# Two unread gaps beside the ring of weights in a two-model float32 kernel

## The chip, the cores and the metric

The kernel runs on one NeuronCore of a Trainium2 chip. The metric is device time in microseconds of one execution, less is better. A time is the median of several runs; for the kernel before, three runs gave 3114.55 us (3114.27 to 3118.92).

## The reference, cut to what matters

Two stacks of two layers each work on one sequence of 256 rows of 1024 numbers in float32. A layer of the first stack is a gated feed-forward block, a mixer with four branches (two convolutions, two kinds of attention), and another feed-forward block; a layer of the second is a feed-forward block, a mixer with windowed attention and a gated delta rule, and another feed-forward block. What is computed around this change is always the same:

```python
normed = norm(h)                         # 256 x 1024
f = (silu(normed @ w_gate) * (normed @ w_up)) @ w_down
u = normed @ w_in                        # some 9,000 columns, then the mixers
```

## The kernel before, in words

Every product with weights is made from three matmuls of a reduced float32 form (float32r). A weight w is held as a high part and a low part (w minus high), an activation likewise, and the product is high x high + high x low + low x high; PARTS in line 1258 is this list.

All weights come through a ring of four slots (SLOTS, UNIT: 2048 floats, 8192 bytes per partition). SyncE loads a unit into a slot of `weight_ring` when TensorE has given the slot back (line 1064, semaphore slots_free). ScalarE copies it, rounded, into the same slot of `weights_high` (line 1837, called from split_high). VectorE, for some units GpSimd, subtracts that from the ring and writes the difference in place, under the name `weights_low` (lines 2177 and 1144): `weight_ring` and `weights_low` are one stretch of memory. Then TensorE reads both parts. Each engine's instructions stand in an order fixed when the program is built, by a plan (PLANS) that also says how far ahead the parts of the next units are made.

The normed rows stand transposed in `normed_t_high` and `normed_t_low` (XT), 8 blocks of 256 columns. Most matmuls multiply a 128x128 block of weights, held stationary in the array after a weight load (LDWEIGHTS), with 256 moving columns of the normed rows. That is so in `cols_product` (line 1264, gate and up), `product` (line 1431, the wide projections) and line 1655 (gates of the branches). In lines 1313 and 1448 the roles are exchanged: the normed rows are stationary, the weights move. In lines 1658 and 1661 the weights are stationary and the moving columns lie in `work_parts`, the split outputs of the mixers. In lines 1373 and 1399 (the down projections) blocks of `work_parts` are stationary and 512 columns of weights move.

A row of the profile names the moving operand first, and then the stationary one: `psum<-normed_t_high,weights_low` has moving normed rows and a stationary block of the low part.

Memory is given out in the order of the declarations, so the places are known. Within a partition (in bytes): `residual` 8192, `normed_t_high` 8192, `normed_t_low` 8192, `weight_ring` (= `weights_low`) 32768, `weights_high` 32768, `feature_rows` 8192, `params` 1916 rounded up to 1920, `constants` 7680, `small` 2128 rounded up to 2144, and `work` (= `work_parts`) 102400. Before the change the normed rows, the low and the high parts start at the same place modulo 512 bytes, and blocks of them are 512 or 1024 bytes long; `work` starts 480 bytes further (8192 + 1920 + 7680 + 2144 = 19936, which is 38 x 512 + 480).

Of the kernel before, what the change touches and what calls it, by code (L numbers as in the profile page):

```python
# [13 lines left out]
P = 128  # L14
# [728 lines left out]
def build_kernel(nc, x, stream1, stream2, prms, feat1, feat2, con, onehot, rowmask, relb, toep, out):  # L743
    with ExitStack() as ctx:
        def sb(name, shape):
            return ctx.enter_context(nc.sbuf_tensor(name, shape, F32))

        def sb_twice(name, parts, shape):


            with nc.sbuf_tensor(name, shape, F32) as whole:
                pass
            return whole, ctx.enter_context(nc.sbuf_tensor(parts, shape, F32R))
# [7 lines left out]
        XTL = ctx.enter_context(nc.sbuf_tensor("normed_t_low", [P, KB, S], F32R))  # L761
        XT = (XTH, XTL)

        RING, LOW = sb_twice("weight_ring", "weights_low", [P, SLOTS, UNIT])
        HIGH = ctx.enter_context(nc.sbuf_tensor("weights_high", [P, SLOTS, UNIT], F32R))
        PG = sb("feature_rows", [P, 2, D])
        PRM = sb("params", [P, max(NCOL1, NCOL2)])
# [195 lines left out]
        def reach(key, k):  # L963
            done = sum(LAYERS[b] * PLANS[b].count.get(key, 0) for b in range(now.blk))
            return CREDIT.get(key, 0) + done + now.l * PLANS[now.blk].count.get(key, 0) + k
# [35 lines left out]
        def loaded_at(i):  # L1001

            return reach(("slot", i % SLOTS), 16 * (i // SLOTS + 1))

        def low_sem(i):
            pl, i, _ = unit_plan(i)
            return low_by_pool if pl.by[i] == "pool" else low_by_vector

        def low_at(i):
            pl, i, following = unit_plan(i)  # L1010
            name = "low_by_" + pl.by[i]
            return reach(name, pl.low_at[i] + following * PLANS[now.blk].count.get(name, 0))

        def some(tile, i, q, n):
            w = width(i) // QUARTERS
            return tile[:, i % SLOTS, q * w:(q + n) * w]
# [59 lines left out]
        def _(pool):  # L1076
# [60 lines left out]
            def split_low(i, q, n):  # L1137

                if low_sem(i) is low_by_pool:
                    pool.wait_ge(high_ready, reach("high_ready", QUARTERS * i + q + n))  # L1140
                    w = width(i) // QUARTERS // 2
                    for part in range(2 * q, 2 * (q + n)):
                        at = (slice(None), i % SLOTS, slice(part * w, (part + 1) * w))
                        ins = pool.tensor_tensor(LOW[at], RING[at], HIGH[at].bitcast(F32), ALU.subtract)  # L1144
                        if part % 2:
# [87 lines left out]
        def _(pe):  # L1233
# [14 lines left out]
            def weights(st, a, wait=True):  # L1248

                i = PLANS[now.blk].place[st.unit]  # L1250
                if wait:
                    pe.wait_ge(low_sem(i), low_at(i))
                n = width(i)
                return [v.rearrange("p (a b) -> p a b", a=a)
                        for v in (HIGH[:, i % SLOTS, 0:n], LOW[:, i % SLOTS, 0:n])]

# [120 lines left out]
            def last_rows(st, t, u, key, stop):  # L1377
# [14 lines left out]
                if t == 0:  # L1392
                    pe.wait_ge(low_sem(i), low_at(i))
                w = [v[:, i % SLOTS, :].rearrange("p (a b) -> p a b", a=2) for v in (HIGH, LOW)]
                for n in range(2):
# [439 lines left out]
        def _(act):  # L1835
            def copy(dst, src, scale=1.0):
                return act.activation(dst, src, ACT.Copy, scale=scale)  # L1837
# [13 lines left out]
            def split_high(i, q, n):  # L1851

                act.wait_ge(slot_loaded[i % SLOTS], loaded_at(i))
                copy(some(HIGH, i, q, n), some(RING, i, q, n)).then_inc(high_ready, n)

# [303 lines left out]
        def _(dve):  # L2159
# [13 lines left out]
            def split_low(i, q, n):  # L2173

                if low_sem(i) is low_by_vector:
                    dve.wait_ge(high_ready, reach("high_ready", QUARTERS * i + q + n))
                    dve.tensor_tensor(some(LOW, i, q, n), some(RING, i, q, n), some(HIGH, i, q, n).bitcast(F32),  # L2177
                                      ALU.subtract).then_inc(low_by_vector, n)
# [647 lines left out]
```

## Time and profile before

| What | Value |
|---|---|
| median of three runs | 3114.55 us |
| span of the profiled execution, first to last instruction | 3111.1 us |
| TensorE matmul busy | 2998.3 us (96%), 22114 matmuls |
| TensorE weight load busy | 2829.8 us (91%) |
| VectorE / ScalarE / GpSimd busy | 61% / 43% / 17% |
| DMA, queue of the weights | 43.0% of 16 engines, 471.95 MB |
| mean granted TensorE clock | 0.991 |

The profiled execution has no time of its own beside its span; the median of the runs is 3.4 us above the span. Matmuls are pipelined: the 0.28 us shown for one matmul is how long it is under way, while its successor starts after 0.12 us. What counts is therefore the step from one start to the next in the timeline.

### The profile page before, as it was taken

To read this page: it belongs to the slowest core of one execution; us is meant where nothing else is said; L and a number is where in the kernel's file an instruction comes from. 1 tells how busy PE (TensorE), PEld (TensorE's weight loads), DVE (VectorE), ACT (ScalarE), POOL (GpSimd) and SP (SyncE) were. 2 spreads that over 40 slices of the span, in tenths; PEclk is the share of its full clock that TensorE was granted. 3 is DMA by queue.
4 is the path that set the end of the run, shared out by engine and by line. 5 is a ranking of instruction groups with operands and counts; after the bars stand their busy time and mean duration, and the time that the engine had idled before them with its cause. 6 is when DMAs were issued, how large, how long until landed. Compare 5 with 4: busy or idle time off the path is not lost.

```text
span 3111.1 us, 54768 instructions
## 1 busy us (share of the span) xinstructions
PE 2998.3 (96%) x22114; PEld 2829.8 (91%) x22114; DVE 1909.5 (61%) x3367; ACT 1348.0 (43%) x2281; POOL 522.1 (17%) x821
## 2 busy tenths in 40 slices
PE   7999999999999999999999998999999999899998
PEld 7999999898999999898998888989989888889897
DVE  5557876656556876655655467466565556664655
ACT  4345454434334454434434543434343355443432
POOL 1000000000000000000002554550000056556000
PEclk9999999999999999999999999999999999999999
DMA  6554445555554456554563322255545533123553
GB/s 226 181 185 163 144 146 180 188 188 181 185 175 177 142 171 176 195 188 176 197 217 136 105 86 77 79 185 180 201 173 216 183 109 109 69 82 137 179 196 130
DMA packets 72861, 498.66 MB, mean 160 GB/s; under 512 B 8320, under 2 KB 8496, under 8 KB 19872
## 3 DMA queue, kind: packets, MB, share of 16 engines
q1 hardware_dynamic: 67824, 471.95, 43.0%
q0 software_dynamic: 4512, 22.20, 2.4%
q8 instruction: 176, 2.88, 0.4%
q10 hardware_dynamic: 272, 0.99, 0.1%
q14 instruction: 77, 0.63, 0.1%
HBM read 490.92 MB, written 4.19 MB: 159 GB/s over the span
## 4 chain that ended last, share of the span: by engine, by line
issue 47%; PE 37%; DVE 7%; POOL 3%; ACT 2%; DVEq 1%; DMA 1%; POOLq 1%; ACTq 0%
PE psum L1264 11%; PE psum L1431 7%; PE psum L1373 4%; PE psum L1655 4%; POOL weights_low L1144 2%; PE psum L1313 2%; DMA weight_ring<-stream 1%; PE psum L1658 1%; PE psum L1661 1%; DVE work L2580 1%; PE psum L1399 1%; DVE weights_low L2177 1%; PE psum L1551 1%; ACT weights_high L1837 1%; PE psum L1771 1%
## 5 line engine op out<-in xcount | busy, mean ns | idle before, releaser
L1837 ACT ACTIVATE weights_high<-weight_ring 128x2048 fp32r<-128x2048 f32 (+5 forms) x774 | 907.5, 1189 | 851.0 <-DMA weight_ring<-stream 850.8
L2177 DVE TENSOR_TENSOR weights_low<-weight_ring,weights_high 128x2048 fp32r<-128x2048 f32 (+5 forms) x528 | 896.4, 1704 | 612.7 <-ACT weights_high L1837 610.5
L1264 PE MATMUL psum<-normed_t_high,weights_high 128*128 128x256 f32 x2560 | 725.1, 283 | 0.0
L1264 PE MATMUL psum<-normed_t_high,weights_low 128*128 128x256 f32 x2560 | 723.9, 283 | 0.0
L1264 PE MATMUL psum<-normed_t_low,weights_high 128*128 128x256 f32 x2560 | 723.9, 283 | 0.0
L1264 PEld LDWEIGHTS psum<-normed_t_high,weights_high 128*128 128x128 f32 x2560 | 490.6, 192 | 3.6 <-issue 0.6
L1264 PEld LDWEIGHTS psum<-normed_t_low,weights_high 128*128 128x128 f32 x2560 | 490.7, 192 | 3.0
L1264 PEld LDWEIGHTS psum<-normed_t_high,weights_low 128*128 128x128 f32 x2560 | 490.7, 192 | 0.0
L1144 POOL TENSOR_TENSOR weights_low<-weight_ring,weights_high 128x256 fp32r<-128x256 f32 x544 | 400.8, 767 | 230.9 <-ACT weights_high L1837 230.8
L1431 PE MATMUL psum<-normed_t_high,weights_high 128*128 128x256 f32 x1248 | 384.4, 308 | 9.2 <-DVE weights_low L2177 9.2
L1431 PE MATMUL psum<-normed_t_low,weights_high 128*128 128x256 f32 x1248 | 355.1, 285 | 0.0
L1431 PE MATMUL psum<-normed_t_high,weights_low 128*128 128x256 f32 x1248 | 354.5, 284 | 0.0
L1373 PE MATMUL psum<-weights_high,work_parts 128*128 128x512 f32 x1088 | 341.7, 395 | 0.0
L1431 PEld LDWEIGHTS psum<-normed_t_high,weights_high 128*128 128x128 f32 x1248 | 241.3, 193 | 22.6 <-issue 16.4
L1431 PEld LDWEIGHTS psum<-normed_t_low,weights_high 128*128 128x128 f32 x1248 | 241.6, 194 | 0.8
L1431 PEld LDWEIGHTS psum<-normed_t_high,weights_low 128*128 128x128 f32 x1248 | 240.6, 193 | 0.0
L1373 PEld LDWEIGHTS psum<-weights_high,work_parts 128*128 128x128 f32 x1088 | 199.3, 188 | 43.6
L1655 PE MATMUL psum<-normed_t_high,weights_high 128*128 128x256 f32 x768 | 232.2, 302 | 4.0 <-POOL weights_low L1144 4.0
L1655 PE MATMUL psum<-normed_t_low,weights_high 128*128 128x256 f32 x768 | 217.5, 283 | 0.0
L1655 PE MATMUL psum<-normed_t_high,weights_low 128*128 128x256 f32 x768 | 217.3, 283 | 0.0
L1373 PE MATMUL psum<-weights_low,work_parts 128*128 128x512 f32 x544 | 214.9, 395 | 0.0
L1399 PE MATMUL psum<-weights_high,work_parts 128*128 128x512 f32 x576 | 182.0, 397 | 0.4 <-DVE weights_low L2177 0.4
(279 smaller groups left out, 4578.5 us busy)
## 6 DMA issues: line engine op xcount, KB each, us to landing
weight_ring<-stream SPq DMA_DIRECT2D x400, 1024.0 KB, 4.8
weight_ring<-stream SPq DMA_DIRECT2D x64, 768.0 KB, 4.2
feature_rows<-feat POOLq DMA_DIRECT2D x12, 1024.0 KB, 5.2
work<-toeplitz_rows POOLq DMA_DIRECT2D x8, 512.0 KB, 6.6
toeplitz_rows<-work POOLq DMA_DIRECT2D x16, 192.0 KB, 3.9
params<-prms POOLq DMA_DIRECT2D x5, 239.5 KB, 3.0
residual<-x SPq DMA_DIRECT2D x2, 512.0 KB, 4.2
out<-residual SPq DMA_DIRECT2D x4, 256.0 KB, 2.0
```

The lines of the kernel that those rows point to most:

```text
L1144: ins = pool.tensor_tensor(LOW[at], RING[at], HIGH[at].bitcast(F32), ALU.subtract)
L1264: ins = pe.matmul(PS[:, bank, at:at + S], w[a][:, first + k, c * P:(c + 1) * P], src[b][:, k, :], start=(k, m) == (0, 0), stop=(k, m) == ( ...
L1313: ins = pe.matmul(PS[:, job.bank, t * S:(t + 1) * S], XT[low][:, k, t * P:(t + 1) * P], w[part][:, k, :], start=n == 0, stop=n == len(FIRS ...
L1373: ins = pe.matmul(PS[:, b, :], src[c][:, r, t * P:(t + 1) * P], w[a][:, r, n * HALF:(n + 1) * HALF], start=start and m == 0, stop=False, s ...
L1399: ins = pe.matmul(PS[:, b, :], src[c][:, r, t * P:(t + 1) * P], w[a][:, r, n * HALF:(n + 1) * HALF], start=False, stop=stop and (r, m) == ...
L1431: ins = pe.matmul(PS[:, job.bank, c * S:(c + 1) * S], w[i][:, k, c * P:(c + 1) * P], XT[j][:, k, :], start=(k, m) == (0, 0), stop=(k, m) = ...
L1551: ins = pe.matmul(dst, q[:, t * P:(t + 1) * P], k[:, 0:keys], start=True, stop=not extra, skip_group_check=True)
L1655: ins = pe.matmul(PS[:, job.bank, 0:S], w[p][:, r, 0:P], XT[q][:, r, :], start=(r, m) == (0, 0), stop=(r, m) == (KB - 1, 2), skip_group_ch ...
L1658: ins = pe.matmul(PS[:, job.bank, S:2 * S], w[p][:, r, 0:P], y[q][:, r - KB, :], start=(r, m) == (KB, 0), stop=(r, m) == (11, 2), skip_gro ...
L1661: ins = pe.matmul(PS[:, job.bank, S:2 * S], w[p][:, r - KB, P:2 * P], y[q][:, r - KB, :], start=(r, m) == (KB, 0), stop=(r, m) == (15, 2), ...
L1837: return act.activation(dst, src, ACT.Copy, scale=scale)
L2177: dve.tensor_tensor(some(LOW, i, q, n), some(RING, i, q, n), some(HIGH, i, q, n).bitcast(F32), ALU.subtract).then_inc(low_by_vector, n)
```

## The change

Two tensors are declared that nothing writes or reads. The first, 8 floats (32 bytes) per partition, stands between the normed rows and the ring; the second, 24 floats (96 bytes), between the ring and the high parts. No instruction is added, removed or moved.

```diff
         XT = (XTH, XTL)
 
+        sb("gap_before_ring", [P, 8])
         RING, LOW = sb_twice("weight_ring", "weights_low", [P, SLOTS, UNIT])
+        sb("gap_behind_ring", [P, 24])
         HIGH = ctx.enter_context(nc.sbuf_tensor("weights_high", [P, SLOTS, UNIT], F32R))
```

With the gaps the ring and the low parts start 32 bytes later, the high parts and all that stands behind them (feature rows, parameters, constants, `work`) 128 bytes later. `residual` and the normed rows stay. The distance between `work` and the high parts stays too.

## Rows read from the trace of the kernel before

**Rows 1.** The page: busy times and shares; the chain by engine.

```profile
PE 2998.3 (96%) x22114; PEld 2829.8 (91%) x22114; DVE 1909.5 (61%) x3367; ACT 1348.0 (43%) x2281; POOL 522.1 (17%) x821
issue 47%; PE 37%; DVE 7%; POOL 3%; ACT 2%; DVEq 1%; DMA 1%; POOLq 1%; ACTq 0%
```

**Rows 2.** Windows 40 to 180 us: length, busy by engine, clock, DMA.

```profile
40.00:180.00 140.00, 140.00 (x988) 131.20 (x987) 75.98 (x78) 50.70 (x41) 0.00 (x0) 1.00 0.53 188
```

**Rows 3.** Groups by line: matmuls of weights and normed rows.

```profile
L1264 PE MATMUL psum<-normed_t_high,weights_high 128*128 128x256 f32 x2560 | 725.1, 283 | 0.0
L1431 PE MATMUL psum<-normed_t_high,weights_high 128*128 128x256 f32 x1248 | 384.4, 308 | 9.2 <-DVE weights_low L2177 9.2
L1655 PE MATMUL psum<-normed_t_high,weights_high 128*128 128x256 f32 x768 | 232.2, 302 | 4.0 <-POOL weights_low L1144 4.0
L1313 PE MATMUL psum<-weights_high,normed_t_high 128*128 128x256 f32 x352 | 55.3, 302 | 6.3 <-DVE normed_t_high L2203 4.6 <-issue 1.6
L1448 PE MATMUL psum<-weights_high,normed_t_high 128*128 128x256 f32 x64 | 18.6, 291 | 0.0
```

**Rows 4.** Timeline of TensorE, line 1264: start, length; first and last of 144.

```profile
49.83 0.28 PE L1264 MATMUL psum<-normed_t_high,weights_high 128*128 128x256 f32 x1
...
66.98 0.28 PE L1264 MATMUL psum<-normed_t_high,weights_low 128*128 128x256 f32 x1
```

**Rows 5.** Timeline of TensorE, line 1661: first and last of 48 matmuls.

```profile
2026.56 0.40 PE L1661 MATMUL psum<-work_parts,weights_high 128*128 128x256 f32 x2
...
2032.12 0.28 PE L1661 MATMUL psum<-work_parts,weights_low 128*128 128x256 f32 x1
```

**Rows 6.** Timeline of TensorE, line 1448: first and last of 36 matmuls.

```profile
341.06 0.28 PE L1448 MATMUL psum<-weights_high,normed_t_high 128*128 128x256 f32 x1
...
345.26 0.28 PE L1448 MATMUL psum<-weights_low,normed_t_high 128*128 128x256 f32 x1
```

**Rows 7.** Groups of weight loads: busy, mean ns of one, idle before.

```profile
L1264 PEld LDWEIGHTS psum<-normed_t_high,weights_low 128*128 128x128 f32 x2560 | 490.7, 192 | 0.0
L1658 PEld LDWEIGHTS psum<-work_parts,weights_high 128*128 128x128 f32 x512 | 78.8, 189 | 0.3
L1373 PEld LDWEIGHTS psum<-weights_high,work_parts 128*128 128x128 f32 x1088 | 199.3, 188 | 43.6
```

**Rows 8.** Timeline of TensorE where line 1264 follows line 1373.

```profile
72.69 0.28 PE L1264 MATMUL psum<-normed_t_high,weights_high 128*128 128x256 f32 x1
72.82 0.28 PE L1264 MATMUL psum<-normed_t_low,weights_high 128*128 128x256 f32 x1
...
73.64 0.28 PE L1264 MATMUL psum<-normed_t_high,weights_low 128*128 128x256 f32 x1
...
74.12 0.28 PE L1264 MATMUL psum<-normed_t_high,weights_high 128*128 128x256 f32 x1
```

**Rows 9.** Windows 1690 to 2030 us, line 1431 and then line 1655 alone.

```profile
1690.00:2030.00 340.00, 149.77 (x963) 124.73 (x961) 0.99 0.26 91
1690.00:2030.00 340.00, 41.33 (x240) 32.38 (x240) 0.99 0.26 91
```

**Rows 10.** Timeline of TensorE, line 1373: first and last of 24 matmuls.

```profile
67.10 0.62 PE L1373 MATMUL psum<-weights_high,work_parts 128*128 128x512 f32 x2
...
72.46 0.40 PE L1373 MATMUL psum<-weights_low,work_parts 128*128 128x512 f32 x1
```

**Rows 11.** Timeline of TensorE, line 1491: 22 steps between these starts.

```profile
216.06 0.25 PE L1491 MATMUL psum<-work_parts,normed_t_low 128*128 128x8 f32 x1
...
218.52 0.25 PE L1491 MATMUL psum<-work_parts,normed_t_high 128*128 128x8 f32 x1
```

**Rows 12.** Loads of weights (KB, us to landing), and their split.

```profile
weight_ring<-stream SPq DMA_DIRECT2D x400, 1024.0 KB, 4.8
L1837 ACT ACTIVATE weights_high<-weight_ring 128x2048 fp32r<-128x2048 f32 x328 | 627.9, 1914 | 823.5 <-DMA weight_ring<-stream 823.3
L2177 DVE TENSOR_TENSOR weights_low<-weight_ring,weights_high 128x2048 fp32r<-128x2048 f32 x314 | 725.8, 2312 | 578.5 <-ACT weights_high L1837 576.4 <-issue 1.6
```

## The prediction, made before the changed kernel ran

> **What bounds the kernel now.** I read the page first: TensorE is busy for 96% of the span, and on the chain that ended last "issue" and PE together hold 84% [rows 1]. "Issue" is time in which TensorE waited for nothing that the profile shows, so this is a kernel whose length is the number of matmuls times the step from one to the next. The windows confirm it for a dense stretch: from 40 to 180 us TensorE is busy for 140.00 of 140 us at a granted clock of 1.00, while VectorE and ScalarE are each busy for about half of it or less [rows 2]. A change that adds no instruction can then act only through that step, through a wait that it creates, or not at all. So the views to read are the groups by line, for how many matmuls have which operands, and the timeline, for their step.
>
> The step is not the same everywhere, although the instructions are. On 256 moving columns of normed rows with a stationary block of weights, 144 matmuls of line 1264 start between 49.83 and 66.98 us: 17.15 us over 143 steps, 119.9 ns [rows 4]. With the same stationary weights, the same shape and 256 moving columns from `work_parts`, 48 matmuls of line 1661 take 5.56 us over 47 steps, 118.3 ns [rows 5]. Where the roles are exchanged and weights move past stationary normed rows, 36 matmuls of line 1448 take 4.20 us over 35 steps, 120.0 ns again [rows 6]. What differs is where the moving columns lie: normed rows start at the same place modulo 512 bytes as the weights, `work` 480 bytes beside them, so that weights stand 32 bytes past the moving columns modulo 512. The weight loads tell the same two cases apart: 192 ns for one in line 1264, 189 in line 1658, 188 in line 1373, whose operands also lie 480 bytes apart [rows 7]. And the slow step is something the engine falls into: where line 1264 follows line 1373, the first eight steps take 0.95 us (118.8 ns each, the first 0.13), and only then does every step take 0.12 [rows 8].
>
> My reading is that the weight load of the next matmul and the moving columns of the present one are read at the same time, and that with equal addresses modulo 512 the two settle into a rhythm that costs 1.6 ns a step. That is a theory: between lines 1264 and 1661 the place of the moving tile itself changes too.
>
> **The change, part by part.** Both gaps cost nothing by themselves: no instruction, no DMA, no wait. What they move:
>
> *Weights against normed rows.* The groups give 3 x (2560 + 1248 + 768 + 352 + 64) = 14,976 matmuls of 256 columns that join weights and normed rows, three for each row shown because of the three parts [rows 3]. In two of three the weight is a high part, whose distance from the normed rows becomes 128 bytes instead of 0; in one it is a low part, now 32 bytes off. Of the 14,976, those in the two stretches of the delta rule, 1690 to 2030 us and an equal one in the second layer, don't run in rows of any length: small matmuls that wait for other engines stand between them, and their step is set there. That is 963 + 240 in the first stretch [rows 9], so about 2,400 in both, and 12,570 are left.
>
> The saving per step is bounded from both sides. The best step that TensorE shows with a 128x128 weight load of this form is 111.8 ns (line 1491, 2.46 us over 22 steps, where only 8 columns move and the load alone sets the pace [rows 11]); that would give 8.1 ns a step, 102 us. The worst is a step that is longer than 119.9: the longest that I see in an undisturbed row is 0.13 between 72.69 and 72.82 us [rows 8], which as a lasting step would cost about 4 ns, 50 us (the timeline rounds to 10 ns, so the 4 is an estimate, from 0.13 less rounding). I take 118.3 ns, because line 1661 is the nearest row: same shape, same weights, another distance. 12,570 x 1.63 ns = 20.4 us less.
>
> This needs the rhythm to be broken for all three parts, though only the low part gets the distance of 32 bytes that a row shows. I count all three, because eight steps pass before the slow rhythm is reached [rows 8], and a low part comes every third. If only the steps of the low parts gain, it is 6.8 us.
>
> *Matmuls with `work`.* High parts and `work` move together. Low parts come 96 bytes further from `work`: in lines 1658 and 1661 one of three matmuls (256 in each, half as many as the 512 with high parts [rows 7]) has a distance that no row shows, and in lines 1373 and 1399 the low parts are the moving operand of one of three: 544 in line 1373 (half of 1,088 [rows 7]) and 288 in line 1399 by the same count. Their step is 233.0 ns now (5.36 us over 23 [rows 10]). If these fell into a rhythm of 120 ns per 256 columns, it would cost 512 x 1.7 ns + 832 x 7 ns = 6.7 us. No row suggests a gain here (233.0 is 116.5 per 256, the best for long moving rows). I take 0.
>
> *Loads and splits.* The ring's rows start 32 bytes off their old place, and the load, the copy on ScalarE and the subtraction on VectorE go there. They take 4.8, 1.9 and 2.3 us a unit [rows 12], 9.0 in all. A slot's next unit is needed three units after the slot comes free, 3 x 48 x 0.12 = 17.3 us, so 8 us of growth per unit are hidden: a landing time that more than doubled would still be covered. Without that cover each us of growth beyond it would cost TensorE 1 us a unit, of which there are 400 of this size. ScalarE and VectorE wait for the stage before them for 823 and 576 us of the span [rows 12], so both have room in the dense stretches. I take 0; a loss begins only behind those 8 us, and a gain would only lengthen waits of ScalarE and VectorE.
>
> *The stretches of the delta rule.* A shorter step among the 2,400 gives at most 2,400 x 1.6 = 4 us, and most of these matmuls come first after an interruption, where the slow rhythm isn't reached. I take 0.
>
> Sum, against the profiled execution: 3111.1 - 20.4 = 3090.7 us of span. The median of the runs shown stands 3.4 us above this span, and nothing in the change touches what lies around it, so 3094.
>
> The Trainium skill has a rule against all this. Its page "TensorE: Matmul & The Clock Gate", section "Step-by-step: what each phase is for", says that TensorE has two independent read ports, one for the moving operand and one for weight loads, and that loading the next block takes no read bandwidth from the running matmul. By that rule addresses would not matter, and the sum would be 3114.5. The two steps of 119.9 and 118.3 ns speak against it, but they don't settle it, since more than the distance differs between them.
>
> **Rivals.**
>
> *Nothing changes.* Either the step depends on the moving tile's own place (the normed rows stay where they are), or on the distance modulo so few bytes that 32 and 128 are both like 0. For it: no row has a distance of 128, and line 1448 shows that exchanging the roles alone leaves the step at 120.0 ns [rows 6]. Against: a place alone would not explain why the slow rhythm takes eight steps to form [rows 8], and the distance of 32 is the one at which line 1661 runs. Time: 3114.5. That the change only half works, on the low parts alone, belongs between the two: 3111.1 - 6.8 + 3.4 = 3107.7.
>
> *A larger gain.* If the new distances free the weight load altogether, the step goes towards 111.8 ns [rows 11]. Half of that way from 118.3, 115 ns, gives 12,570 x 4.9 = 62 us, 3053. Against: no long row of 256 columns that I found is faster than 118.3 ns, and the rows of 512 columns show 116.5 per 256 with loads that fill only half of their time.
>
> *A worse rhythm.* The pair at 128 bytes for two parts and 32 for the third settles into a step above 119.9. Place: line 1264 and line 1431, which run in rows of 100 and more. Price: 122 ns costs 12,570 x 2.1 = 26 us, 3141, and with the 512-column matmuls of the low parts up to 3147. It is slower than now from the point where the mean step exceeds 119.9, or where the loss of up to 6.7 us on `work` is larger than the gain. For it: single steps of 0.13 occur after a change of operands [rows 8]. Against: with the one other distance that the trace shows, every row is quicker.
>
> **How the numbers follow.** Chances: the forecast 0.44 (all parts gain, 3084 to 3102), half an effect 0.10 (3102 to 3108), a larger gain 0.12 (below 3084), nothing 0.20, a worse rhythm 0.14. What a measurement of this kernel can tell from no change is about 0.2%, 6 us. Faster by more: 0.44 + 0.12 + 0.10 = 0.66; within: 0.20; slower by more: 0.14. The range reaches from 3054, which takes in the larger gain down to a step of about 115 ns, to 3122, which holds no change and the first third of the slower case; some 0.08 is left out below and 0.10 above.
>
> **What would show it.** Right: in the timeline of the changed kernel, 144 matmuls of line 1264 take under 17.0 us, and the weight loads of line 1264 fall from a mean of 192 ns towards 189; lines 1661 and 1373 keep their steps. The low-part theory alone shows as every third step shorter. No change shows as 0.12 in every step and 192 ns. A worse rhythm shows as steps of 0.12 and 0.13 mixed, and the loads above 192. If the loads of the ring land later than 4.8 us and TensorE begins to wait for weights_low, the cover that I counted was not there. The prediction is wrong if line 1264 keeps its step while the span moves, or if its step falls and the span doesn't.

## The result, and the profile after

The changed kernel takes 3092.06 us (median of three runs, 3091.88 to 3094.23) against 3114.55: a ratio of 0.9934 with a 95% interval of 0.992 to 0.9948, 22.5 us less. The prediction was 3094. The profiled execution took 3094.23 us, 3092.4 of them in its span; the span before was 3111.1, so 18.7 us are to be found in the two traces. Line numbers are two higher than before from the ring's declaration on.

The page and the window of 40 to 180 us answer to [rows 1, 2]: first the busy times, then the shares of the chain, and below them the window (length, then busy time and count of PE, PEld, DVE, ACT and POOL, granted clock, DMA share, GB/s).

```profile
PE 2976.1 (96%) x22114; PEld 2813.3 (91%) x22114; DVE 1911.1 (62%) x3367; ACT 1347.6 (44%) x2281; POOL 521.3 (17%) x821
issue 48%; PE 36%; DVE 7%; POOL 3%; ACT 2%; DVEq 2%; DMA 1%; POOLq 1%; ACTq 0%
```
```profile
40.00:180.00 140.00, 140.00 (x1001) 131.68 (x1000) 75.97 (x78) 51.36 (x42) 0.00 (x0) 1.00 0.53 188
```

The same instructions on every engine, and shares of the chain that differ from before by one point at most. But in the same 140 us, without a gap and at the same granted clock of 1.00, there are 1001 matmuls where there were 988: 13 more, 1.3%. So in this window the change is a shorter step, and nothing else.

The timeline of TensorE shows it: start, length, then line and operands; the first and the last of the 144 matmuls that answer to [rows 4].

```profile
49.62 0.28 PE L1266 MATMUL psum<-normed_t_high,weights_high 128*128 128x256 f32 x1
...
66.56 0.28 PE L1266 MATMUL psum<-normed_t_high,weights_low 128*128 128x256 f32 x1
```

16.94 us over 143 steps is 118.5 ns; it was 119.9. The groups of weight loads of this line and of the two that answer to [rows 7] (busy us, mean ns of one, idle before):

```profile
L1266 PEld LDWEIGHTS psum<-normed_t_high,weights_low 128*128 128x128 f32 x2560 | 483.3, 189 | 0.0
L1660 PEld LDWEIGHTS psum<-work_parts,weights_high 128*128 128x128 f32 x512 | 78.8, 188 | 0.3
L1375 PEld LDWEIGHTS psum<-weights_high,work_parts 128*128 128x128 f32 x1088 | 199.2, 188 | 41.4
```

In line 1266, 192 ns have become 189; line 1660 has 188 where it had 189, and line 1375 its 188 as before. Where blocks of `work_parts` are stationary and 512 columns of weights move, the 24 matmuls that answer to [rows 10] are these, with the first three starts and the last:

```profile
66.68 0.63 PE L1375 MATMUL psum<-weights_high,work_parts 128*128 128x512 f32 x2
67.15 0.39 PE L1375 MATMUL psum<-weights_low,work_parts 128*128 128x512 f32 x1
67.37 0.63 PE L1375 MATMUL psum<-weights_high,work_parts 128*128 128x512 f32 x2
...
72.00 0.40 PE L1375 MATMUL psum<-weights_low,work_parts 128*128 128x512 f32 x1
```

5.32 us over 23 steps, 231.3 ns; it was 233.0. This step was to stay, and it did not. The step of line 1663 (1661 before) did stay: 24 matmuls, 2.72 us over 23 steps, 118.3 ns, as in [rows 5].

```profile
2024.39 0.40 PE L1663 MATMUL psum<-work_parts,weights_high 128*128 128x256 f32 x2
...
2027.11 0.28 PE L1663 MATMUL psum<-work_parts,weights_low 128*128 128x256 f32 x1
```

The ring and its split answer to [rows 12] (KB and us to landing; then busy us, mean ns, idle before):

```profile
weight_ring<-stream SPq DMA_DIRECT2D x400, 1024.0 KB, 4.8
```
```profile
L1839 ACT ACTIVATE weights_high<-weight_ring 128x2048 fp32r<-128x2048 f32 x328 | 628.4, 1916 | 810.5 <-DMA weight_ring<-stream 810.5
L2179 DVE TENSOR_TENSOR weights_low<-weight_ring,weights_high 128x2048 fp32r<-128x2048 f32 x314 | 731.7, 2331 | 564.9 <-ACT weights_high L1839 562.8 <-issue 1.6
```

Landing and copy are as before, the subtraction 1% longer. TensorE waits for low parts in line 1433 for 9.7 us where it waited 9.2 [rows 3], and in line 1315 (1313 before) for 8.2 where it waited 7.3 (line and engine waited for, total us, times, longest; before, then after):

```profile
PE psum L1313 <- DVE weights_low L2177: 7.3, 8, 1.0
PE psum L1315 <- DVE weights_low L2179: 8.2, 8, 1.2
```

To see all rows and not two, I took every step between successive starts of the same kind from both traces, without those over 140 ns (260 for 512 columns), which are interruptions. Moving normed rows past weights: 119.71 ns before (12,602 steps) and 118.54 after (12,575), 14.7 us less. Moving 256 columns of weights past normed rows: 119.74 and 118.43 (1,097 steps), 1.4 us. Moving `work_parts` past weights: 118.29 and 118.25, nothing. Moving 512 columns of weights past `work_parts`: 233.24 and 231.26 (2,393), 4.7 us. Together 20.8 us, against 18.7 us of span. Of the 2.1 between, 1.4 us are the two waits just named; the rest is less than one execution differs from the next by.

### The profile page after: what moved, and what is told of

It reads as the page before. It is cut to its first block, busy times and chain, and to the rows that moved or that the text cites. A ratio compares the mean times of both kernels' runs of the same rounds, so it can differ in the third digit from the quotient of the medians.

```text
span 3092.4 us, 54768 instructions
## 1 busy us (share of the span) xinstructions
PE 2976.1 (96%) x22114; PEld 2813.3 (91%) x22114; DVE 1911.1 (62%) x3367; ACT 1347.6 (44%) x2281; POOL 521.3 (17%) x821
## 4 chain that ended last, share of the span: by engine, by line
issue 48%; PE 36%; DVE 7%; POOL 3%; ACT 2%; DVEq 2%; DMA 1%; POOLq 1%; ACTq 0%
PE psum L1266 11%; PE psum L1433 6%; PE psum L1375 4%; PE psum L1657 4%; POOL weights_low L1146 2%; PE psum L1315 2%; PE psum L1660 1%; DMA weight_ring<-stream 1%; PE psum L1663 1%; DVE weights_low L2179 1%; DVE work L2582 1%; PE psum L1553 1%; PE psum L1401 1%; ACT weights_high L1839 1%; PE psum L1773 1%
## 5 line engine op out<-in xcount | busy, mean ns | idle before, releaser
L1266 PEld LDWEIGHTS psum<-normed_t_high,weights_high 128*128 128x128 f32 x2560 | 481.2, 188 | 3.7 <-issue 0.6
L1266 PEld LDWEIGHTS psum<-normed_t_low,weights_high 128*128 128x128 f32 x2560 | 481.5, 188 | 3.1
L1266 PEld LDWEIGHTS psum<-normed_t_high,weights_low 128*128 128x128 f32 x2560 | 483.3, 189 | 0.0
L1146 POOL TENSOR_TENSOR weights_low<-weight_ring,weights_high 128x256 fp32r<-128x256 f32 x544 | 399.9, 767 | 233.1 <-ACT weights_high L1839 233.0
L1433 PEld LDWEIGHTS psum<-normed_t_high,weights_high 128*128 128x128 f32 x1248 | 239.5, 192 | 23.2 <-issue 17.3
L1433 PEld LDWEIGHTS psum<-normed_t_low,weights_high 128*128 128x128 f32 x1248 | 239.6, 192 | 0.8
L1433 PEld LDWEIGHTS psum<-normed_t_high,weights_low 128*128 128x128 f32 x1248 | 237.8, 191 | 0.0
```

What stands on the lines that cost most here:

```text
L1266: ins = pe.matmul(PS[:, bank, at:at + S], w[a][:, first + k, c * P:(c + 1) * P], src[b][:, k, :], start=(k, m) == (0, 0), stop=(k, m) == ( ...
L1433: ins = pe.matmul(PS[:, job.bank, c * S:(c + 1) * S], w[i][:, k, c * P:(c + 1) * P], XT[j][:, k, :], start=(k, m) == (0, 0), stop=(k, m) = ...
```

## The experiments

The theory: the step depends on the distance, modulo 512 bytes, between the stationary block that is being loaded and the columns that move. The first rival: on the places themselves. The table holds what all runs gave. Distances are in bytes from the normed rows to the low parts, the high parts and `work`, and then from the high parts to `work`. Steps are means in ns, taken as above: normed rows past weights (256 columns), `work` past weights (256), weights past `work` (512). "Rows" says at what step the 80 rows of gate and up (line 1264 before; 48, 96 or 144 matmuls each) run over their last 24 steps, which nothing interrupts. Steps and rows come from one profiled execution of each kernel; that of e11, 3116.11 us, was its slowest of ten. The ratio is against the kernel before in the same job. The diffs, cut to the lines that matter, are against the changed kernel; those of e7 and e9 are against the kernel before, that of e12 against e9.

| Kernel | low, high, work; high to work | normed past w. | work past w. | w. past work | rows | median us | ratio (95%) |
|---|---|---|---|---|---|---|---|
| before | 0, 0, 480; 480 | 119.71 | 118.29 | 233.24 | 120.0 | 3114.55 | |
| after | 32, 128, 96; 480 | 118.54 | 118.25 | 231.26 | 118.2 to 119.0 | 3092.06 | 0.9934 (0.992 to 0.9948) |
| e1 | 0, 0, 480; 480 | 119.71 | 118.29 | 233.24 | 120.0 | 3111.75 | 0.9995 (0.9985 to 1.0005) |
| e2 | 32, 32, 0; 480 | 118.35 | 118.36 | 233.26 | 118.3 | 3096.52 | 0.9948 (0.9932 to 0.9963) |
| e3 | 0, 128, 96; 480 | 118.40 | 118.20 | 233.21 | 118.3 | 3095.52 | 0.9945 (0.9929 to 0.9961) |
| e4 | 128, 128, 96; 480 | 119.35 | 118.23 | 233.45 | 62 at 120.0, 18 at 118.5 to 118.8 | 3109.36 | 0.9993 (0.9982 to 1.0003) |
| e5 | 32, 32, 96; 64 | 118.34 | 117.50 | 233.20 | 118.3 | 3095.2 | 0.995 (0.9932 to 0.9967) |
| e6 | 64, 64, 96; 32 | 114.89 | 117.02 | 233.12 | 62 at 113.3, 18 at 117.8 | 3056.45 | 0.9822 (0.9804 to 0.9841) |
| e7 | 96, 96, 224; 128 | 118.39 | 118.48 | 232.83 | 75 at 118.5 to 118.8, 5 at 117.2 to 117.4 | 3097.3 | 0.9951 (0.9935 to 0.9966) |
| e8 | 0, 0, 0; 0 | 119.79 | 119.67 | 227.77 | 120.0 | 3101.31 | 0.9965 (0.9953 to 0.9978) |
| e9 | 64, 64, 64; 0 | 116.57 | 118.73 | 226.95 | 71 at 117.8, 9 at 113.3 | 3068.96 | 0.986 (0.9844 to 0.9877) |
| e10 | 192, 192, 160; 480 | 117.49 | 118.22 | 233.07 | 75 at 117.8, 5 at 113.3 | 3086.41 | 0.9919 (0.9905 to 0.9934) |
| e11 | 64, 128, 96; 480 | 119.20 | 118.34 | 233.17 | 64 at 120.0, 14 at 118.7, 2 at 117.8 | 3108.04 | 0.9989 (0.9978 to 0.9999) |
| e12 | e9 and 64 short matmuls | 116.70 | 118.73 | 227.56 | 70 at 117.8, 10 at 113.3 | 3078.02 | 0.9889 (0.9872 to 0.9906) |

**e1: all places moved, no distance changed.** One gap of 8 floats ahead of the normed rows, none at the ring.

```diff
+        sb("gap_before_normed", [P, 8])
         XTH = ...
-        sb("gap_before_ring", [P, 8])
-        sb("gap_behind_ring", [P, 24])
```

> One gap of 32 bytes in front of the normed rows: normed rows, low parts, high parts and work all move by 32 bytes together, so no distance between two of them changes. If the distance between the weight load and the moving columns sets the step, the dense rows stay at a step of 119.9 ns with loads of 192 ns, and the time is that of the kernel before, 3114 within 3 us. If it is the place of a tile by itself (a start at the same place modulo 64 or 128 bytes), the step falls to about 118.5 ns and the time to about 3095.

The time is that of the kernel before within 0.1%, and the three steps of the table are the same to the last digit (weights past normed rows: 119.72 and 119.74). The loads of line 1265 have their old length too:

```profile
L1265 PEld LDWEIGHTS psum<-normed_t_high,weights_low 128*128 128x128 f32 x2560 | 490.7, 192 | 0.0
```

So a shift of all by 32 bytes does nothing: places themselves are ruled out, as far as 32 bytes can show, and distances are left.

**e2: the gap in front alone.** Both parts stand 32 bytes off.

```diff
         sb("gap_before_ring", [P, 8])
-        sb("gap_behind_ring", [P, 24])
```

> Only the gap in front of the ring: low and high parts both stand 32 bytes from the normed rows; weights and work keep their distances. Distance theory: the dense step falls to 118.3 to 118.5 ns as with both gaps (12,570 steps x 1.4 ns = 18 us), the matmuls of 512 columns in line 1373 keep 233 ns, so about 3098. If the gain of the changed kernel needs the high parts at 128, the step stays near 119.9 and the time near 3114.

The first row of 144 and the loads of its line:

```profile
49.46 0.28 PE L1265 MATMUL psum<-normed_t_high,weights_high 128*128 128x256 f32 x1
...
66.38 0.28 PE L1265 MATMUL psum<-normed_t_high,weights_low 128*128 128x256 f32 x1
```
```profile
L1265 PEld LDWEIGHTS psum<-normed_t_high,weights_low 128*128 128x128 f32 x2560 | 482.3, 188 | 0.0
```

16.92 us over 143 steps, 118.3 ns, the value of [rows 5] at the distance that the prediction read from there. The normed rows have not moved, and the 32 bytes by which the weights have moved did nothing in e1, so this is the distance again. `work` has moved too, but e5, where it lies elsewhere, has the same 118.34. With no instruction changed, 32 bytes take 1.36 ns from 12,600 steps, 17 us.

**e3: the high parts alone.** The ring stays; a gap of 32 floats behind it puts the high parts at 128 bytes.

```diff
-        sb("gap_before_ring", [P, 8])
-        sb("gap_behind_ring", [P, 24])
+        sb("gap_behind_ring", [P, 32])
```

> Only a gap of 128 bytes behind the ring: the low parts stay at distance 0 from the normed rows, the high parts go to 128. If breaking the rhythm for one or two of the three parts is enough, the dense step falls to about 118.5 ns, and the low parts, as moving operand against work that is 128 bytes further, change the 512-column step; about 3093 to 3098. If only the low parts' 32 bytes act (128 is like 0), the step stays at 119.9 and the time at 3114 or a little below.

118.40 ns, although the low parts are still at distance 0 in every third matmul. The two halves of the change are therefore not two gains that add: e2 (1.36 ns) and e3 (1.31) each shorten these steps by no less than the whole change does (1.17). What the changed kernel has beyond them is the shorter step of the 512 columns.

**e4: all at 128.**

```diff
-        sb("gap_before_ring", [P, 8])
-        sb("gap_behind_ring", [P, 24])
+        sb("gap_before_ring", [P, 32])
```

> Low and high parts both 128 bytes from the normed rows, weights and work unchanged to each other. If the step depends on the distance modulo 128 bytes or less, nothing changes: 119.9 ns, loads 192 ns, 3114. If the distance counts to more than 128 bytes, the step falls below 119 and the time to 3095 to 3100.

No gain that can be measured. The row of 96 that follows the first down projection:

```profile
72.81 0.28 PE L1265 MATMUL psum<-normed_t_high,weights_high 128*128 128x256 f32 x1
...
84.20 0.29 PE L1265 MATMUL psum<-normed_t_high,weights_low 128*128 128x256 f32 x1
```

11.39 us over 95 steps, 119.9 ns: 128 bytes by itself is as slow as 0, in 62 of 80 rows. In e3 and in the changed kernel the same 128 bytes run at 118.2 to 119.0, beside low parts at 0 or at 32. What decides is thus the row of three parts together, not each matmul's own distance. Nor is this the rhythm of distance 0: read at the trace's 1 ns, the steps of the row shown repeat 117, 120, 123, while at distance 0 each is 120.

**e5: distance 64 for the 512 columns.** In the changed kernel the steps of moving low parts in lines 1375 and 1401 fell to 228.62 ns (741 steps), those of moving high parts only to 232.45 (1,652). Low parts stood 64 bytes from `work`, high parts 480. So both parts at 64 from `work` were to be quick.

```diff
         sb("gap_before_ring", [P, 8])
-        sb("gap_behind_ring", [P, 24])
...
+        sb("gap_before_work", [P, 24])
         W, WP = sb_twice("work", ...)
```

> Low and high parts both 32 bytes from the normed rows (gap of 32 in front of the ring, none behind it), and a gap of 96 bytes in front of work, so that work stands 64 bytes past all weights, as it stands past the low parts in the changed kernel, where the 512-column steps of the low parts take 228.6 ns instead of 233.2. If the distance alone sets the step: dense 118.35 ns (17 us less than before over 12,600 steps), lines 1313 and 1448 117.2 ns (3 us), all 2,390 steps of 512 columns near 228.6 (11 us), together 31 us, about 3082, which beats the changed kernel by 10. If the 228.6 come from having low and high at two different distances, the 512-column steps stay at 233 and the time is that of e2, about 3096.

A miss: 233.56 ns for low and 233.04 for high parts, no gain there. The 512 columns don't follow the distance of the single matmul either.

**e6: the parts at 64.**

```diff
-        sb("gap_before_ring", [P, 8])
-        sb("gap_behind_ring", [P, 24])
+        sb("gap_before_ring", [P, 16])
...
+        sb("gap_before_work", [P, 16])
         W, WP = sb_twice("work", ...)
```

> Low and high parts 64 bytes from the normed rows, work 32 bytes past the weights. If the rhythm repeats every 64 bytes, the dense step is 119.9 ns as at distance 0 and the time about 3112; if every 128 or more, it lies at 118.3 to 118.6 and the time at 3095 to 3099 (the 512-column steps, now at a new distance, may add or take up to 10 us).

The best version, 3056.45 us, a ratio of 0.9822: better than both kernels, and outside both cases of the expectation. The first row of 144, and the row of 96 behind the next down projection:

```profile
49.76 0.28 PE L1266 MATMUL psum<-normed_t_high,weights_high 128*128 128x256 f32 x1
...
66.60 0.28 PE L1266 MATMUL psum<-normed_t_high,weights_low 128*128 128x256 f32 x1
...
72.32 0.28 PE L1266 MATMUL psum<-normed_t_high,weights_high 128*128 128x256 f32 x1
...
83.11 0.28 PE L1266 MATMUL psum<-normed_t_high,weights_low 128*128 128x256 f32 x1
```

16.84 us over 143 steps is 117.8 ns, 10.79 over 95 is 113.6. The same line, operands and distances, and two steps: after its first few matmuls the second row runs at 113.3 to its end. Most rows in this kernel do. The sum over the kinds, (119.71 - 114.89) x 12,600 = 60.7 us and 5.5 for the other kinds, is 10.6 us more than the 55.6 that the span shortened, from 3111.1 to 3055.5: some is given back in waits, as those of TensorE for split weights show (line, engine and line waited for, total us, times, longest):

```profile
PE psum L1433 <- DVE weights_low L2179: 10.8, 4, 2.9
PE psum L1315 <- DVE weights_low L2179: 7.8, 9, 1.0
PE psum L1657 <- POOL weights_low L1146: 6.8, 3, 2.3
```

In the kernel before, these were 9.2, 7.3 and 4.0 us: 4.9 of the 10.6. Where the rest went is not shown.

Which rows get which step is not random. Read at 1 ns, of the 64 rows that follow a down projection the 8 whose first matmul starts 240 ns after the last one of the down projection run at 117.8, and the 56 that start after 232 to 236 ns at 113.3. The 16 rows of 144 are 8 of the one and 8 of the other, with the same operands and distances. So within one kernel the way a row is entered goes with its step; that it causes it is not shown.

**e7: the parts at 96, `work` 128 bytes from them.** As e6, with 24 floats ahead of the ring and 40 ahead of `work`.

```diff
+        sb("gap_before_ring", [P, 24])
...
+        sb("gap_before_work", [P, 40])
```

> Low and high parts 96 bytes from the normed rows, work 128 bytes past the weights. If only the distance modulo 64 counts, the dense step is that of 32 bytes, 118.35 ns, and the 512-column step of line 1373 that of a distance of 64 or 0 modulo 64; time 3082 to 3099. A step of 119.3 or more at 96 bytes would say that no simple period describes it.

118.39 ns, as with 32 bytes. So 64 is better than what stands on either side of it.

**e8: `work` alone, to distance 0.** Parts and normed rows as in the kernel before; only the moving columns of lines 1658 and 1661 (here 1659 and 1662) and the stationary blocks of lines 1373 and 1399 (here 1374 and 1400) move.

```diff
-        sb("gap_before_ring", [P, 8])
-        sb("gap_behind_ring", [P, 24])
...
+        sb("gap_before_work", [P, 8])
```

> Normed rows and weights as before the change; only work moves by 32 bytes, to distance 0 from the weights. If equal addresses make the slow rhythm, lines 1658 and 1661 go from 118.3 to 119.9 ns and their loads from 189 to 192 (1,260 steps, 2 us); if long moving rows fall into it too, line 1373 and 1399 go from 233.2 towards 240 (2,390 steps, up to 16 us): 3115 to 3130. If the moving tile's own place mattered, line 1264 would still be at 119.9 and lines 1658 and 1661 too, without the loads changing.

Half of the theory holds. The 24 matmuls of `work_parts` past weights, and then the 24 of 512 columns:

```profile
2029.91 0.40 PE L1662 MATMUL psum<-work_parts,weights_high 128*128 128x256 f32 x2
...
2032.67 0.28 PE L1662 MATMUL psum<-work_parts,weights_low 128*128 128x256 f32 x1
```
```profile
66.88 0.63 PE L1374 MATMUL psum<-weights_high,work_parts 128*128 128x512 f32 x2
...
72.12 0.39 PE L1374 MATMUL psum<-weights_low,work_parts 128*128 128x512 f32 x1
```

2.76 us over 23 is 120.0 ns: the line that ran at 118.3 has taken up the slow step, as the theory has it for distance 0, and the loads of high parts in line 1659 (1658 before) went from 189 to 192 ns, in line 1662 (1661) only from 190 to 191. But 5.24 us over 23 is 227.8 ns: with 512 columns the same distance is quicker than 480 [rows 10], where it was expected to be slower. 2,393 x 5.5 ns is 13.1 us, which outweighs the 1,256 x 1.4 = 1.7 us lost, and the kernel got faster where a loss or nothing was expected.

**e9: the best of both.** Parts and `work` at 64 from the normed rows, at 0 from each other.

```diff
+        sb("gap_before_ring", [P, 16])
...
+        sb("gap_before_work", [P, 8])
```

> The two best distances together: weights 64 bytes from the normed rows (dense step 114.9 ns in e6 against 119.7 before) and work at distance 0 from the weights (512-column step 227.8 ns in e8 against 233.2). If each distance sets its own step: against e6 2,390 x 5.3 = 12.7 us less, and 1,256 steps of lines 1658 and 1661 at 119.7 instead of 117.0, 3.4 us more, so about 3047, some 45 us faster than the changed kernel. If the 512-column step needs the weights to start at the same place modulo 128 bytes as in e8, it stays at 233 and the time at 3056 to 3060.

A miss by 22 us. The 512 columns took 226.95 ns as hoped, but the row of 96 at the place of that of e6 is this:

```profile
71.78 0.28 PE L1266 MATMUL psum<-normed_t_high,weights_high 128*128 128x256 f32 x1
...
82.96 0.28 PE L1266 MATMUL psum<-normed_t_high,weights_low 128*128 128x256 f32 x1
```

11.18 us over 95 steps, 117.7 ns and not 113.6. For line 1266 nothing differs between e6 and e9: the same operands, at the same places. What differs is `work`, 32 bytes further on in e6, and with it the step of the matmuls that run before the row (and the place of what other engines read and write there meanwhile). All 64 rows behind a down projection start 226 or 227 ns after it here, and all run at 117.8. The loads of the line are no key to it either:

```profile
L1266 PEld LDWEIGHTS psum<-normed_t_high,weights_low 128*128 128x128 f32 x2560 | 490.6, 192 | 0.0
L1266 PEld LDWEIGHTS psum<-normed_t_high,weights_high 128*128 128x128 f32 x2560 | 480.8, 188 | 3.1 <-issue 0.6
```

192 ns for the low parts, as in the kernel before, and 188 for the high parts, at one step of 117.8 ns. In e10, at the same step, the low parts have 188 too:

```profile
L1265 PEld LDWEIGHTS psum<-normed_t_high,weights_low 128*128 128x128 f32 x2560 | 481.3, 188 | 0.0
```

**e10: the parts at 192.**

```diff
-        sb("gap_before_ring", [P, 8])
-        sb("gap_behind_ring", [P, 24])
+        sb("gap_before_ring", [P, 48])
```

> Low and high parts 192 bytes (64 + 128) from the normed rows, weights and work at the old distance to each other. If the pattern repeats every 128 bytes: dense step 114.9 ns as at 64, loads 188, the 512-column steps 233, about 3054 to 3060. If it repeats only at 256 or 512 bytes, the step is somewhere else between 115 and 120, 3060 to 3112.

The steps of the rows are the same two values as with 64, 117.8 in 75 rows and 113.3 in 5. In these kernels the distance goes with the steps that occur, and 64 and 192 have the same pair; which of the two a row gets is another matter. The 64 rows behind a down projection start 227 to 234 ns after it and all run at 117.8, so the first interval alone doesn't decide. That 64 and 192 agree, and 0 and 128 share their 120.0, would suit a period of 128 bytes; but 18 rows at 128 run at 118.5 to 118.8 (e4), and none at 0 does.

**e11: low parts at 64, high parts at 128.** If each part brought its own step, the mean over the three would give a gain.

```diff
-        sb("gap_before_ring", [P, 8])
+        sb("gap_before_ring", [P, 16])
...
-        sb("gap_behind_ring", [P, 24])
+        sb("gap_behind_ring", [P, 16])
```

> Low parts 64 bytes from the normed rows, high parts 128, work 96 (480 past the high parts as before). If each matmul has the step of its own weight load's distance: one of three near 114.9, two near 119.35 as with both at 128, mean 117.9, 12,600 x 1.8 = 23 us less than before, about 3089. If the rhythm of all three follows its best part, 115 to 116, 3065; if two different distances always give the uneven 118.4 to 118.6 of the changed kernel and of e3, about 3094.

A miss for all three cases, the mean among them, which had 3089 us: 3108.04, and 64 of 80 rows at 120.0. With e3 and e4 this shows that parts at different distances don't average. 0 and 128, each slow alone, are quick together; 64, quick alone, is slow together with 128.

**e12: another start for the rows.** e9 with one more matmul of 8 columns ahead of each row of line 1266 that follows a down projection, into the bank that the row then begins anew. If a row's step is chosen by how its first matmuls meet their loads, this could move it to 113.3.

```diff
+                if came_from[0] == "down":
+                    pe.matmul(PS[:, job.bank, 0:8], w[0][:, 0, 0:P], XT[0][:, 0, 0:8], start=True, stop=True, skip_group_check=True)
+                came_from[0] = "gu"
```

> The kernel of e9 with one more small matmul (8 moving columns, into a place that the next matmul overwrites) in front of each row of line 1264 that follows a down projection, 64 rows of 96 or 144 matmuls. In e9 all these rows run at 117.8 ns a step, in e6 most of the same rows at 113.3, though no operand of line 1264 differs between the two. If a row keeps the rhythm into which it starts, some or all rows change to 113.3: up to 64 x 107 x 4.5 = 31 us less for 64 x 0.12 = 8 us more, 3046 to 3069. If the rhythm belongs to the addresses of the whole kernel and not to the start, all rows stay at 117.8 and the time is 3077.

The start of the same row as above:

```profile
71.70 0.17 PE L1357 MATMUL psum<-normed_t_high,weights_high 128*128 128x8 f32 x1
71.72 0.36 PE L1267 MATMUL psum<-normed_t_high,weights_high 128*128 128x256 f32 x1
71.92 0.28 PE L1267 MATMUL psum<-normed_t_low,weights_high 128*128 128x256 f32 x1
```

The second step is 0.20 us instead of 0.12, and the row is at 117.8 all the same, as are all 64 that were given the extra matmul; the time is 3078.02. This disturbance doesn't switch a row; another might.

What stays open: what chooses between 113.3 and 117.8 (the way into the row goes with it in e6, but e12, which changed that way for the rows of e9, switched none); why 512 columns are quick at distance 0 and, for low parts alone, in the changed kernel, but not in e5; and what in the chip makes the distance count. The runs show distances and steps, not the mechanism.

## Why the prediction was right, and where its steps were off

The number was right, by two errors of opposite sign and nearly equal size, so that its closeness is in part luck; the mechanism behind its largest term is confirmed in part.

- *TensorE's step is the only way for this change to act.* Right: the same instructions, 1001 for 988 matmuls in the dense window.
- *The step depends on the distance, not on the place.* Right, and argued only from a few single rows at the time. e1 and e2 show it for 256 columns; e9 shows that the distance is not all.
- *The dense term, 12,570 x 1.63 ns = 20.4 us.* This is the term that was mis-sized: it measured 16.1 us, 14.7 from 12,575 steps of normed rows past weights and 1.4 from 1,097 of weights past normed rows. The count was nearly right: 12,014 uninterrupted steps outside the stretches of the delta rule. They fell from 119.84 to 118.53 ns, 1.31 ns a step instead of 1.63, which is 15.7 us. Both ends had been read from single rows, 119.9 and 118.3, and the second, 118.3, belongs to another distance than two of the three parts got.
- *The stretches of the delta rule, 0.* Right: 1,677 of their steps are uninterrupted, and these only fell from 118.85 to 118.54 ns, 0.5 us.
- *All three parts gain.* Right: the steps up to a matmul with a low part take 118.50 ns, those up to one with a high part 118.56. The low-part rival, every third step shorter, is refuted. The reason given, that the low part breaks the rhythm of its neighbours, is shown only so far that a part can do so: in e3 two parts of three move, to 128, and all gain. That the low part at 32 is what does it in the changed kernel is not shown, and e11 shows that not every mixture of distances breaks the slow step.
- *Matmuls with `work`, 0 with a bound of 6.7 us on the side of a loss.* Failed: a gain of 4.7 us, all in the 512 columns (233.24 to 231.26 ns). The prediction held 233 ns for the best that long moving rows do; e8 has 227.8 and e9 227.0. The bound had only one sign, from a missing row: no row with a smaller step was seen, and that was taken for a reason.
- *Loads and splits, 0.* Right: 4.8 us and 1.9 as before, the waits for low parts in lines 1433 and 1315 1.4 us longer together.
- *The loads fall from 192 to 189.* It came true, but it is no measure of the step: 188 ns go with 118.3 (e2), with 117.8 (e10) and with the 113.3 of most rows of e6, and e9 has 192 and 188 in the same rows.
- *3.4 us outside the span.* That was the difference between a span and a median of other executions. The profiled execution after took 1.8 us beside its span. The kernel before, measured again in four jobs, had medians of 3111.4 to 3112.9, so its 3114.55 lay some 2 us high: the ratio, and the steps, are firmer than the 22.5 us.
- *A larger gain, by half of the way to 111.8 ns.* It did not come here, yet e6 has it: 114.89 ns and 3056 us, where that rival said 115 and 3053. The price, with one end taken from a row of another shape [rows 11], was close.
- *A worse rhythm, above 120 ns.* In no run as a mean. e4 and e11 fall back to 120.0, none beyond, though single steps of 123 and 125 ns recur in their rows.

The rule that the prediction weighed against itself, from the Trainium skill's page "TensorE: Matmul & The Clock Gate", section "Step-by-step: what each phase is for", that loading the next block takes no read bandwidth from the running matmul, would have left the time at 3114.5. The runs disagree with what was taken from it, that addresses don't matter, as far as this form of matmul goes: in e2 only addresses differ, and 12,600 steps are 1.36 ns shorter. That it is the read ports which meet is not shown.

## What to carry to other kernels

Where TensorE is busy without a gap and "issue" leads the chain, count the matmuls in a fixed window and compare the step of lines with equal shapes but different operands: a difference of one per cent between them may be the relative place of stationary and moving operand, and an unread gap of 32 to 192 bytes is all it takes to try. Try several distances on the chip, first with all parts of a product at the same one, since mixed distances don't average, and look at every long row: in this kernel the values gathered at a few steps. Take a step's size from all steps of its kind, not from one row of the timeline.

## What was not expected of the hardware

- A long row settles near one of a few mean steps: 120.0, 118.2 to 119.0, 117.2 to 117.8 or 113.3 ns for 256 columns. With all parts at one distance, 0 showed only the first, 32 only 118.3, 64 and 192 only 117.8 and 113.3, 128 only 120.0 and 118.5 to 118.8, and 96 118.5 to 118.8 and 117.2 to 117.4.
- Between 118 and 119 ns the steps of a row are not equal. Read at 1 ns over their last 60 steps, the rows of 96 and 144 repeat 8 steps of 115 to 123 ns in e2 and 12 steps of 112 to 124 in e3, to within 1 ns; at distance 0 every step is 119 or 120, and in such rows at 113.3 every one is 113 or 114.
- The same 96 matmuls at the same places take 113.6 ns each in e6 and 117.7 in e9; what differs is 32 bytes in the place of `work`, and so what runs before and beside them.
- Equal places modulo 512 are the slowest case for 256 columns (120.0 ns) and the quickest seen for 512 (227.8 and 227.0 ns).
- Unread memory, 128 bytes of each partition, is worth more than twice this change: 64 bytes ahead of the ring and 64 ahead of `work` (e6) took 1.8% from a kernel whose TensorE was already busy for 96% of its span.
